# A hybrid encoder block on one core: some steps of the gated recurrence are put at other places between the projection groups

## The chip, the cores and the metric

The kernel runs on one core of a Trainium2 chip. The metric is the device time of one execution in microseconds (us); lower is better.

## The reference

One layer of a streaming encoder, for x of 2048 positions by 1024 features in f32:

```python
h = _rmsnorm(x, norm1_w[layer])
proj = h @ w_in[layer]                      # 1024 x 2816
qa, ka, va, qb, fb, ib, gb = jnp.split(proj, SPLIT_POINTS, axis=-1)
ya = _swa_sink_attention(qa, ka, va, ...)   # 8 query heads, 2 key heads, band of 128
yb = _hgrn2(qb, fb, ib, gb, ...)            # 4 heads of a gated linear recurrence
x = x + jnp.concatenate([ya, yb], axis=-1) @ w_out[layer]
h = _rmsnorm(x, norm2_w[layer])
gate, up = jnp.split(h @ w_gate_up[layer], 2, axis=-1)
x = x + (jax.nn.silu(gate) * up) @ w_down[layer]
```

The change is in the part of `_hgrn2`. Per head it makes, for chunks of 64 positions:

```python
b = jnp.cumsum(jnp.log(fg), axis=3)
att = einsum(qh * exp(b - ref), kh * exp(ref - b))    # causal scores inside a chunk
d_state = einsum(kh * exp(b_last - b), vh)            # what each chunk adds to the state
state = decay * state + d_state                       # a scan over the chunks
o = _rmsnorm(att @ vh + (qh * exp(b)) @ state, g_norm_w) * silu(g)
```

## The kernel before

There are two phases. The first (0 to about 885 us) computes the projection, the banded attention, the recurrence and the output projection; the second is the feed-forward part, and the change leaves it alone.

The first phase goes through 4 blocks of 512 positions (`b` = 0 to 3). A block is one list of steps, `STEPS`, made by `block_steps`. Its backbone is the projection: weight chunks with the names KV, QA0, QA1, F0, F1, Q01, I01, G01, F23, Q23, I23, G23, then WO0 to WO3 for the output projection. Each chunk is cut in 2 or 4 groups; a group is 24 matmuls on TensorE (L208 to L210, eight tiles with three products each) into one of two banks `a_pj`. The call `after(chunk, group, steps...)` lists by hand what comes between one group and the next. Below "G01,3" is group 3 of chunk G01.

Every engine has a loop of its own over the same list, and does its share of each step in this order. An engine never takes a later step first: if its instruction waits, all that is listed behind it waits too. The steps of the recurrence for a head h, and who works in them:

- `ha`: VectorE scales the gate (L952), ScalarE takes its logarithm (L605).
- `hb`: VectorE makes the running sum and the differences (L956, L958, L961, L966), then ScalarE five exponentials (L610 to L615).
- `hc`: VectorE four products (L971, L972, L974, L975). `kt` and `att` of the head wait for the last of them.
- `kt`: TensorE transposes `a_k_end` into a bank `a_tr` (L814), ScalarE copies it to `a_k_nat` (L651).
- `ds` (listed twice for a head, because it fills two banks; the work is done at the second): TensorE makes the state increments from `a_k_nat` and `a_i_nat` (L826), and VectorE scans them into `a_state` and `a_carry`: a copy (L1015) and eight dependent instructions that read the banks (L1019).
- `att`: TensorE makes the scores into `a_hb` (L806), VectorE copies them masked into `a_att_m` (L1011).
- `o`: TensorE multiplies scores and state by the values (L833, L838). `on1`, `on2`, `on3` normalize, `yt` transposes the result.

Of the attention there are: `sm1` (softmax: maxima on VectorE, L984 to L989, exponentials on ScalarE, L634 and L636), `sm2` (the division on VectorE, L993 to L997), `pt` (TensorE transposes the probabilities, L787, ScalarE copies them, L642) and `pv` (TensorE, L797; ScalarE L646, VectorE L1002). The weights of a chunk are rounded by ScalarE (`split_hi`, L518), and VectorE makes what is left (`split_lo`, L855). Where they have no place of their own in the list, those of the next chunk stand ahead of group 0 for the chunks of two groups, F23 among them, and behind it for the chunks of four. The evacuation of each projection group is ScalarE's, in the step of the group itself (L576 for F, L578 for Q, L581 for G, L591 for I).

The steps `qT`, `pt`, `kt`, `ds`, `yt` and `xT` take turns in two banks `a_tr`, in the order of the list. Ahead of each, TensorE waits until the bank has been read by whoever uses it two turns earlier; for `ds` that reader is the scan, which tells it with its last instruction:

```python
def bank_read(b, use):
    if use >= 2:
        read, index = tr_read[TR_USES[use - 2][0]]
        pe.wait_ge(read.sem, read.upto(b, index(TR_USES[use - 2])))

tr_read = {..., "pt": (probT_ready, ...), "kt": (k_nat_ready, ...), "ds": (state_ready, ...), ...}
```

And `ds` waits for the copy of the keys and for the values, which for heads 2 and 3 means all four groups of chunk I23:

```python
if par == 0:
    pe.wait_ge(k_nat_ready.sem, k_nat_ready.upto(b, h + 1))
    pe.wait_ge(i_ready.sem, i_ready.upto(b, TT if h < 2 else 2 * TT))
bank_read(b, use)
```

The loads of weights on SyncE's queue wait for `split_lo` of two chunks earlier. GpSimd has the small powers for the normalizations, and some loads and stores.

Of the kernel before, what the change touches and what calls it, by code (L numbers as in the profile page):

```python
# [57 lines left out]
def chunk_name(n):  # L58
    return CHUNKS[n][0] if n < len(CHUNKS) else f"WO{n - len(CHUNKS)}"


def chunk_groups(n):

    name = chunk_name(n)
    return CHUNKS[n][2] // P if name in FIRST_HEAD else TT
# [4 lines left out]
CHUNK_AT = {chunk_name(n): n for n in range(NW)}  # L70


def block_steps():

    at = {}

    def after(name, group, *steps):
        at.setdefault((name, group), []).extend(steps)

    after("KV", 3, ("vmix",))
    after("QA1", 0, ("qn1", 0))
    after("QA1", 1, ("qn1", 1))
    after("QA1", 2, ("qn1", 2), ("qn2", 0))
    after("QA1", 3, ("qn1", 3))
    after("F0", 0, ("qn2", 1), ("split_hi", CHUNK_AT["Q01"]), ("split_lo", CHUNK_AT["Q01"]), ("qn2", 2))
    after("F1", 0, ("qn2", 3))
    after("Q01", 0, ("qT", 0), ("qT", 1), ("qT", 2), ("qT", 3), ("kT",))  # L90
    after("Q01", 1, ("sc", 0), ("sm1", 0), ("sm1", 1))
    after("I01", 0, ("ha", 0), ("split_hi", CHUNK_AT["G01"]))
    after("I01", 1, ("sm2", 0), ("sm2", 1), ("sc", 1), ("split_lo", CHUNK_AT["G01"]))
    after("I01", 2, ("pt", 0), ("pt", 1), ("sm1", 2), ("sm1", 3), ("hb", 0))
    after("I01", 3, ("sm2", 2), ("sm2", 3), ("pv", 0), ("sc", 2))
    after("G01", 0, ("pt", 2), ("pt", 3), ("sm1", 4), ("sm1", 5), ("xload",), ("hc", 0), ("ha", 1))
    after("G01", 1, ("sm2", 4), ("sm2", 5), ("pv", 1), ("split_hi", CHUNK_AT["F23"]), ("split_lo", CHUNK_AT["F23"]))
    after("G01", 2, ("pt", 4), ("pt", 5), ("sc", 3), ("att", 0), ("kt", 0), ("sm1", 6), ("sm1", 7), ("hb", 1))
    after("G01", 3, ("ds", 0, 0), ("ds", 0, 1), ("sm2", 6), ("sm2", 7), ("pv", 2), ("hc", 1))
    after("F23", 0, ("pt", 6), ("pt", 7))  # L100
    after("F23", 1, ("pv", 3), ("o", 0), ("on1", 0), ("kt", 1), ("ha", 2), ("sq", 0))
    after("Q23", 0, ("on2", 0), ("on3", 0), ("hb", 2), ("split_lo", CHUNK_AT["I23"]), ("ds", 1, 0), ("ds", 1, 1), ("att", 1))
    after("Q23", 1, ("yt", 0), ("hc", 2), ("sq", 1))
    after("I23", 0, ("o", 1), ("on1", 1), ("ha", 3))
    after("I23", 1, ("on2", 1), ("on3", 1), ("split_lo", CHUNK_AT["G23"]), ("kt", 2), ("sq", 2))
    after("I23", 2, ("yt", 1), ("att", 2), ("sq", 3))
    after("I23", 3, ("hb", 3),)
    after("G23", 0, ("ds", 2, 0), ("ds", 2, 1), ("hc", 3), ("n1a",))
    after("G23", 1, ("o", 2), ("on1", 2), ("kt", 3), ("n1b", 0), ("n1b", 1))
    after("G23", 2, ("on2", 2), ("ds", 3, 0), ("ds", 3, 1), ("att", 3))  # L110
    after("G23", 3, ("on3", 2), ("o", 3), ("on1", 3), ("yt", 2), ("n1b", 2), ("on2", 3), ("on3", 3), ("n1b", 3))
    for n in range(CHUNK_AT["WO0"], NW):
        after(chunk_name(n), 1, ("split_lo", n + 1))
    after("WO0", 0, ("xT", 0))
    after("WO0", 1, ("xT", 1))
    after("WO0", 2, ("xT", 2))
    after("WO1", 0, ("xT", 3))
    after("WO1", 2, ("xT", 4))
    after("WO2", 0, ("xT", 5))
    after("WO2", 2, ("xT", 6))  # L120
    after("WO3", 0, ("xT", 7))

    placed = [step for group in at.values() for step in group if step[0].startswith("split")]
    steps = []
    for n in range(NW):
        first_steps = [part for part in (("split_hi", n + 1), ("split_lo", n + 1)) if part not in placed]
        for g in range(chunk_groups(n)):
            if (chunk_name(n), g) == ("WO0", 0):
                first_steps.append(("yt", HG - 1))
            if g == 0 and (chunk_groups(n) < TT or chunk_name(n) == "WO0"):  # L130
                steps += first_steps
            steps.append(("proj", n, g))
            steps += at.pop((chunk_name(n), g), [])
            if g == 0 and not (chunk_groups(n) < TT or chunk_name(n) == "WO0"):
                steps += first_steps
    assert not at, at
    return steps


STEPS = block_steps()  # L140


# [1475 lines left out]
```

## Time and profile before

| | us |
|---|---|
| median of 3 runs | 2302.94 (2302.03 to 2303.75) |
| the profiled execution | 2303.67 |
| its span, first to last instruction | 2301.9 |
| TensorE busy | 2199.6 |
| VectorE busy | 1261.1 |
| ScalarE busy | 928.7 |
| mean granted TensorE clock | 0.984 |

The span is the time in which the profile shows instructions; the time of the execution has 1.8 us more around it. "Busy" counts the time in which an instruction of the engine runs. Start times below are counted from the beginning of the span, and the four blocks of the first phase look alike: the same step lies some 218 us later in the next block.

### The profile page before, as it was taken

What the parts mean: (1) busy time and instruction counts of PE and PEld (TensorE: products, weight loads), DVE (VectorE), ACT (ScalarE), POOL (GpSimd) and SP (SyncE); (2) the same over time, 40 slices, a digit from 0 to 9 for tenths busy, and PEclk for the clock granted to TensorE, in tenths of its full rate; (3) what the DMA queues carried; (4) which work ended last, traced back from release to release, by engine and by line L of the source; (5) the groups of instructions that cost most, each with busy time, mean ns of one, the idle gap of its engine ahead of it and who ended that gap; (6) DMA issues with size and microseconds to landing.
All of it is one profiled execution on the core that took longest, in us unless ns stands there. A gap on an engine that the chain in (4) does not pass through costs nothing.

```text
span 2301.9 us, 31427 instructions
## 1 busy us (share of the span) xinstructions
PE 2199.6 (96%) x12640; PEld 1903.9 (83%) x12640; DVE 1261.1 (55%) x1902; ACT 928.7 (40%) x1674; POOL 143.9 (6%) x154
## 2 busy tenths in 40 slices
PE   7999999999999993699999999999999999999999
PEld 7889988998898893588888888888888788888887
DVE  4675466447635754556666566555555334343333
ACT  4773386448535741333333333333333222232222
POOL 2001201010112002100000000000000000000000
PEclk9999999999999997799999999999999999999999
DMA  3412332323133125623334233222221435445453
GB/s 133 146 58 102 119 112 74 129 92 112 56 138 119 56 93 189 240 84 133 133 133 151 83 137 119 83 82 83 83 83 65 150 139 187 178 180 186 172 193 134
DMA packets 81648, 284.00 MB, mean 123 GB/s; under 512 B 8608, under 2 KB 17056, under 8 KB 66912
## 3 DMA queue, kind: packets, MB, share of 16 engines
q1 hardware_dynamic: 67296, 221.96, 27.2%
q0 software_dynamic: 14208, 60.04, 7.1%
q8 instruction: 100, 1.64, 0.3%
q14 instruction: 44, 0.36, 0.0%
HBM read 227.44 MB, written 54.53 MB: 122 GB/s over the span
## 4 chain that ended last, share of the span: by engine, by line
PE 58%; DMA 2%; DVE 1%; issue 0%; DVEq 0%; POOL 0%; ACT 0%; SPq 0%; POOLq 0%
PE b_bank_A L209 3%; PE b_bank_A L208 3%; PE b_bank_C L209 3%; PE b_bank_B L209 3%; PE b_bank_B L208 3%; PE b_bank_B L210 3%; PE b_bank_A L210 3%; PE b_bank_C L208 3%; PE b_bank_C L210 3%; PE b_hx_bank L1400 3%; PE b_hx_bank L1402 3%; PE b_hx_bank L1401 3%; PE b_bank_D L208 2%; PE b_bank_D L209 2%; PE b_bank_D L210 2%; PE b_hx_bank L1349 1%
## 5 line engine op out<-in xcount | busy, mean ns | idle before, releaser
L1418 DVE TENSOR_TENSOR b_dn_lo<-b_dn_stage,b_dn_hi 128x1024 fp32r<-128x1024 f32 x88 | 107.8, 1226 | 303.8 <-ACT b_dn_hi L1302 303.7
L208 PE MATMUL a_pj<-a_w_hi,a_hT_hi 128*128 128x256 f32 x896 | 259.0, 289 | 1.7 <-issue 1.7
L209 PE MATMUL a_pj<-a_w_lo,a_hT_hi 128*128 128x256 f32 x896 | 253.3, 283 | 0.0
L210 PE MATMUL a_pj<-a_w_hi,a_hT_lo 128*128 128x256 f32 x896 | 253.3, 283 | 0.0
L1302 ACT ACTIVATE b_dn_hi<-b_dn_stage 128x1024 fp32r<-128x1024 f32 x88 | 93.3, 1060 | 341.8 <-PE b_bank_D L1402 310.6
L208 PEld LDWEIGHTS a_pj<-a_w_hi,a_hT_hi 128*128 128x128 f32 x896 | 171.6, 191 | 6.8 <-issue 4.4
L855 DVE TENSOR_TENSOR a_w_lo<-a_w_stage,a_w_hi 128x2048 fp32r<-128x2048 f32 (+1 forms) x64 | 137.9, 2155 | 71.2 <-ACT a_w_hi L518 71.2
L209 PEld LDWEIGHTS a_pj<-a_w_lo,a_hT_hi 128*128 128x128 f32 x896 | 171.7, 192 | 0.0
L210 PEld LDWEIGHTS a_pj<-a_w_hi,a_hT_lo 128*128 128x128 f32 x896 | 171.6, 191 | 0.0
L1400 PE MATMUL b_hx_bank<-b_dn_hi,b_a_hi 128*128 128x512 f32 x352 | 138.3, 393 | 4.9 <-DVE b_a_lo L1418 4.8
L1402 PE MATMUL b_hx_bank<-b_dn_hi,b_a_lo 128*128 128x512 f32 x352 | 137.9, 392 | 0.0
L1401 PE MATMUL b_hx_bank<-b_dn_lo,b_a_hi 128*128 128x512 f32 x352 | 137.9, 392 | 0.0
L208 PE MATMUL b_bank_A<-b_h_hi_B,b_w_hi 128*128 128x512 f32 x352 | 137.6, 391 | 0.0
L208 PE MATMUL b_bank_B<-b_h_hi_T,b_w_hi 128*128 128x512 f32 x352 | 137.3, 390 | 0.0
L209 PE MATMUL b_bank_A<-b_h_lo_B,b_w_hi 128*128 128x512 f32 x352 | 137.2, 390 | 0.0
L210 PE MATMUL b_bank_A<-b_h_hi_B,b_w_lo 128*128 128x512 f32 x352 | 137.0, 389 | 0.0
L210 PE MATMUL b_bank_B<-b_h_hi_T,b_w_lo 128*128 128x512 f32 x352 | 137.0, 389 | 0.0
L209 PE MATMUL b_bank_B<-b_h_lo_T,b_w_hi 128*128 128x512 f32 x352 | 136.9, 389 | 0.0
L1335 ACT ACTIVATE b_gate<-b_u 128x512 f32<-128x512 f32 x44 | 27.8, 632 | 241.3 <-DVE b_u L1541 241.3
L518 ACT ACTIVATE a_w_hi<-a_w_stage 128x2048 fp32r<-128x2048 f32 (+1 forms) x64 | 115.3, 1801 | 1.5 <-DMA a_w_stage<-w_whole 1.5
L1418 DVE TENSOR_TENSOR b_w_lo<-b_mixed_w,b_w_hi 128x1024 fp32r<-128x1024 f32 x88 | 107.6, 1222 | 11.5 <-ACT b_w_hi L1277 11.5
L1321 ACT ACTIVATE b_s<-b_bank_C 128x512 f32<-128x512 f32 x44 | 26.4, 600 | 206.3 <-PE b_bank_C L210 206.3
(266 smaller groups left out, 5557.6 us busy)
## 6 DMA issues: line engine op xcount, KB each, us to landing
a_w_stage<-w_whole SPq DMA_DIRECT2D x56, 1024.0 KB, 4.7
b_gu_stage<-w_gu SPq DMA_DIRECT2D x44, 1024.0 KB, 5.2
b_dn_stage<-w_dn SPq DMA_DIRECT2D x88, 512.0 KB, 3.4
a_mid<-b_a SPq DMA_DIRECT2D x88, 256.0 KB, 4.1
b_a_stage<-a_mid SPq DMA_DIRECT2D x88, 256.0 KB, 3.6
b_hx<-hc POOLq DMA_DIRECT2D x14, 1024.0 KB, 5.1
a_x_res<-x_pad POOLq DMA_DIRECT2D x16, 512.0 KB, 4.4
x_mid<-a_x_res POOLq DMA_DIRECT2D x16, 512.0 KB, 3.4
```

Source lines behind the costliest of these rows:

```text
L208: pe.matmul(out, stationary[0](k), moving[0](k), start=(k == 0 and not adds), stop=False, skip_group_check=adds)
L209: pe.matmul(out, stationary[0](k), moving[1](k), start=False, stop=False, skip_group_check=adds)
L210: last = pe.matmul(out, stationary[1](k), moving[0](k), start=False, stop=(k == ends), skip_group_check=adds)
L518: act.activation(w_hi[s][:, :, 0:cols], w_stage[s][:, :, 0:cols], ACT.Copy).then_inc(w_hi_ready.sem, 1)
L855: dve.tensor_tensor(w_lo[s][:, :, 0:cols], w_stage[s][:, :, 0:cols], w_hi[s][:, :, 0:cols].bitcast(F32), ALU.subtract).then_inc(w_lo_ready ...
L1302: act.activation(f.dn_hi[b][:], f.dn_stage[b][:], ACT.Copy).then_inc(f.dn_hi_ready, 1)
L1321: act.activation(f.s5[:], f.bank["C"][:], ACT.Copy).then_inc(f.s5_ready, 1)
L1335: act.activation(f.gate[1][:], f.u2[:], ACT.Silu).then_inc(f.silu_ready[1], 1)
L1400: pe.matmul(f.down[i], f.a_hi[b][:, rows], f.dn_hi[b][:, cols], start=(j == 0), stop=False)
L1401: pe.matmul(f.down[i], f.a_hi[b][:, rows], f.dn_lo[b][:, cols], start=False, stop=False)
L1402: last = pe.matmul(f.down[i], f.a_lo[b][:, rows], f.dn_hi[b][:, cols], start=False, stop=(j == FT - 1))
L1418: dve.tensor_tensor(out, full, hi.bitcast(F32), ALU.subtract).then_inc(ready, 1)
```

## The change

Five steps move in the list of a block; nothing is added or taken out.

- `kt` of head 0 goes from behind G01,2 to behind G01,3.
- `ds` of head 0 goes from behind G01,3 to behind F23,0, where it stands ahead of `pt` 6 and 7.
- `att` of head 1 goes from behind Q23,0 to behind Q23,1.
- `ds` of head 2 goes from behind G23,0 to behind I23,3, where it stands ahead of `hb` of head 3.

```diff
-    after("G01", 2, ("pt", 4), ("pt", 5), ("sc", 3), ("att", 0), ("kt", 0), ("sm1", 6), ("sm1", 7), ("hb", 1))
-    after("G01", 3, ("ds", 0, 0), ("ds", 0, 1), ("sm2", 6), ("sm2", 7), ("pv", 2), ("hc", 1))
-    after("F23", 0, ("pt", 6), ("pt", 7))
+    after("G01", 2, ("pt", 4), ("pt", 5), ("sc", 3), ("att", 0), ("sm1", 6), ("sm1", 7), ("hb", 1))
+    after("G01", 3, ("kt", 0), ("sm2", 6), ("sm2", 7), ("pv", 2), ("hc", 1))
+    after("F23", 0, ("ds", 0, 0), ("ds", 0, 1), ("pt", 6), ("pt", 7))
     after("F23", 1, ("pv", 3), ("o", 0), ("on1", 0), ("kt", 1), ("ha", 2), ("sq", 0))
-    after("Q23", 0, ("on2", 0), ("on3", 0), ("hb", 2), ("split_lo", CHUNK_AT["I23"]), ("ds", 1, 0), ("ds", 1, 1), ("att", 1))
-    after("Q23", 1, ("yt", 0), ("hc", 2), ("sq", 1))
+    after("Q23", 0, ("on2", 0), ("on3", 0), ("hb", 2), ("split_lo", CHUNK_AT["I23"]), ("ds", 1, 0), ("ds", 1, 1))
+    after("Q23", 1, ("att", 1), ("yt", 0), ("hc", 2), ("sq", 1))
     after("I23", 0, ("o", 1), ("on1", 1), ("ha", 3))
     after("I23", 1, ("on2", 1), ("on3", 1), ("split_lo", CHUNK_AT["G23"]), ("kt", 2), ("sq", 2))
     after("I23", 2, ("yt", 1), ("att", 2), ("sq", 3))
-    after("I23", 3, ("hb", 3),)
-    after("G23", 0, ("ds", 2, 0), ("ds", 2, 1), ("hc", 3), ("n1a",))
+    after("I23", 3, ("ds", 2, 0), ("ds", 2, 1), ("hb", 3),)
+    after("G23", 0, ("hc", 3), ("n1a",))
```

## Rows read from the trace of the kernel before

**Rows 1.** The page's busy times: us, share of the span, instructions.

```profile
PE 2199.6 (96%) x12640; PEld 1903.9 (83%) x12640; DVE 1261.1 (55%) x1902; ACT 928.7 (40%) x1674; POOL 143.9 (6%) x154
```

**Rows 2.** TensorE's waits, first phase: line <- releaser: us in all, times, longest.

```profile
PE a_tr L787 <- DVE a_prob L997: 4.4, 8, 0.9
PE a_tr L814 <- ACT a_probT L642: 3.7, 4, 1.1
...
PE a_hb L833 <- DVE a_carry L1019: 2.9, 4, 0.7
...
PE a_tr L814 <- DVE a_q_h L975: 1.7, 4, 0.7
```

**Rows 3.** Timeline of TensorE, block 1, head 0: start, us, what [idle before <-releaser].

```profile
325.82 1.16 PE L806 MATMUL a_hb<-a_q_in,a_f_gate 128*128 128x128 f32 x8
328.09 0.63 PE L814 MATMUL a_tr<-ident,a_k_end 128*128 128x128 f32 x4 [1.11 <-ACT a_probT L642]
331.51 1.16 PE L826 MATMUL a_tr<-a_i_nat,a_k_nat 64*128 64x128 f32 x16
...
339.94 0.66 PE L787 MATMUL a_tr<-ident,a_prob 128*128 128x128 f32 x4 [0.58 <-DVE a_prob L997]
...
341.44 0.48 PE L208 MATMUL a_pj<-a_hT_hi,a_w_hi 128*128 128x512 f32 x1
```

**Rows 4.** Timeline of VectorE over the same stretch.

```profile
335.18 0.22 DVE L1015 COPY a_state<-a_carry 128x128 f32<-128x128 f32 x1
...
338.45 0.35 DVE L1019 SCALAR_TENSOR_TENSOR a_carry<-a_state,a_decay,a_tr 128x128 f32<-128x128 f32 x1
...
340.89 0.68 DVE L1002 TENSOR_TENSOR a_yA_lo<-a_pv,a_yA_hi 128x512 fp32r<-128x512 f32 x1
...
344.06 2.29 DVE L855 TENSOR_TENSOR a_w_lo<-a_w_stage,a_w_hi 128x2048 fp32r<-128x2048 f32 x1
```

**Rows 5.** Timeline of ScalarE over the same stretch.

```profile
339.37 0.59 ACT L646 ACTIVATE a_yA_hi<-a_pv 128x512 fp32r<-128x512 f32 x1
339.85 1.91 ACT L518 ACTIVATE a_w_hi<-a_w_stage 128x2048 fp32r<-128x2048 f32 x1
```

**Rows 6.** Timeline of TensorE, block 1, heads 2 and 3.

```profile
382.61 1.16 PE L826 MATMUL a_tr<-a_i_nat,a_k_nat 64*128 64x128 f32 x16
...
387.56 1.13 PE L833 MATMUL a_hb<-a_i_nat,a_att_m 128*128 128x128 f32 x8 [0.73 <-DVE a_carry L1019]
...
390.05 0.66 PE L814 MATMUL a_tr<-ident,a_k_end 128*128 128x128 f32 x4 [0.33 <-DVE a_q_h L975]
...
395.65 1.13 PE L806 MATMUL a_hb<-a_q_in,a_f_gate 128*128 128x128 f32 x8 [1.00 <-DVE a_y_nat L1029]
```

**Rows 7.** Timeline of ScalarE over the same stretch.

```profile
379.84 0.39 ACT L591 ACTIVATE a_i_nat<-a_pj 128x256 f32<-128x256 f32 x1 [1.62 <-PE a_pj L210]
381.26 0.63 ACT L610 ACTIVATE a_q_in<-a_t_a 128x512 f32<-128x512 f32 x1 [1.04 <-DVE a_k_end L966]
...
383.13 0.61 ACT L615 ACTIVATE a_t_b<-a_t_b 128x512 f32<-128x512 f32 x1
```

**Rows 8.** Timeline of VectorE over the same stretch.

```profile
378.32 0.41 DVE L956 TENSOR_SCALAR a_f_gate<-a_f_gate 128x512 f32<-128x512 f32 x1
...
380.55 0.68 DVE L966 TENSOR_TENSOR a_k_end<-a_t_b 128x512 f32<-128x512 f32 x1
383.82 0.23 DVE L1015 COPY a_state<-a_carry 128x128 f32<-128x128 f32 x1 [2.59 <-PE a_tr L826]
...
387.33 0.69 DVE L971 TENSOR_TENSOR a_q_in<-a_q_in,a_q_h 128x512 f32<-128x512 f32 x1
```

**Rows 9.** A window: length, busy PE PEld DVE ACT POOL, granted clock, DMA share, GB/s.

```profile
1820.00:1840.00 20.00, 15.17 (x56) 12.05 (x55) 5.48 (x6) 4.73 (x6) 0.00 (x0) 0.83 0.52 196
```

**Rows 10.** Timeline of TensorE inside that window.

```profile
1826.79 0.77 PE L1400 MATMUL b_hx_bank<-b_dn_hi,b_a_hi 128*128 128x512 f32 x1 [4.83 <-DVE b_a_lo L1418]
...
1832.05 0.50 PE L1400 MATMUL b_bank_A<-b_dn_hi,b_a_hi 128*128 128x512 f32 x1
```

## The prediction

> **What bounds the kernel now.** I read the page's busy times first: TensorE works 2199.6 of 2301.9 us, VectorE little more than half of it [rows 1]. So almost everything that the other engines do is hidden, and a change of order counts only through what TensorE waits for. I therefore read TensorE's waits in the first phase. Those at places that the change touches are small: the transposes of the probabilities (L787) wait 4.4 us in all, `kt` 3.7 us for the bank and 1.7 us for the products of `hc`, `o` 2.9 us for the scan [rows 2]. Third, the timelines of block 1 put them in their places: `kt` 0 waits 1.11 us behind `att` 0, and `pt` 6 waits 0.58 us behind group F23,0 [rows 3]; `o` of head 2 waits 0.73 us, `kt` 3 waits 0.33 us, `att` 3 waits 1.00 us [rows 6]. The reader is to see how short these are, and that VectorE and ScalarE are nonetheless packed nearly without a break just there: from 335.2 to 346.35 us VectorE has one piece of work behind the other [rows 4]. A step that is put late into such a queue ends late, and the question for each move is who then waits for its end.
>
> **Head 0: what is removed.** `kt` 0 no longer stands behind `pt` 5, so its wait of 1.11 us a block goes (0.9 on the average: 3.7 in 4 [rows 2]). TensorE then reaches the end of group F23,0 early: `att` 0 begins at 325.82 and takes 1.16, `kt` 0 with G01,3 take 331.51 - 328.09 = 3.42, and `pv` 2 with F23,0 take 339.94 - 0.58 - 331.51 - 1.16 = 6.69 us [rows 3]. That makes 337.1 us.
>
> **Head 0: what is added.** Now come `ds` 0, `pt` 6 and `pt` 7 with no group between them. `pt` 6 and 7 take the two banks that `ds` 0 has just filled, and `bank_read` makes them wait for `state_ready`, thus for the last instruction of the scan. Before, the whole of F23,0 lay between. So the time of `pt` 6 is the end of the scan, and that is a matter of VectorE's queue, which I work out row by row.
>
> - ScalarE: behind the evacuation of G01,3 its copy of `kt` 0 is put in. The copy that follows in the list, of the same 512 columns out of a bank, takes 0.59 us and its successor starts 339.85 - 339.37 = 0.48 later [rows 5]; I take 0.52. The copy for `pv` 2 then ends at 339.37 + 0.52 + 0.59 = 340.5 us.
> - `ds` 0 on TensorE waits for this key copy, which is done at about 340.0. TensorE is idle from 337.1 to 340.0, and `ds` ends at 341.2 (1.16 us [rows 3]). This is not the last wait.
> - VectorE: the scan is gone from its place at 335.18, so `sm2` is done early, but `pv` 2 (L1002) must wait for ScalarE's 340.5. It began at 340.89 before [rows 4], so all that follows comes 0.4 us earlier: the four products of `hc` 1, and the `split_lo` of Q23, which stands ahead of group F23,0 in the list and ended at 344.06 + 2.29 = 346.35; now 345.95. Only then comes the scan, from its copy to its last instruction 338.45 + 0.35 - 335.18 = 3.62 us [rows 4]. It ends at 349.6. The `split_lo` itself waits for ScalarE's `split_hi`, 0.5 us later than before, at 339.85 + 0.52 + 1.91 = 342.3, and that is in time.
>
> `pt` 6 then starts near 349.7. Before, from `pt` 6 to F23,1 went 341.44 - 339.94 = 1.50 us, of which about 0.5 was a second wait, for the probabilities of `pt` 7 (4.4 / 4 less 0.58 [rows 2, 3]), that is long over now; I take off 0.2 more, as transposes that wait for nothing overlap, and reach 350.5. F23,1 began at 341.44: it is 9.0 us late, and this already counts the wait that was removed. What comes after in `STEPS` had no wait until `o` of head 2 and is TensorE's own work; nothing gives the 9.0 us back. The four blocks are alike: 36.0 us.
>
> **Head 1.** `att` 1 moves behind Q23,1. VectorE's list is the same as before there, and its masked copy is an instruction like L1002, some 0.7 us [rows 4]. `o` 1 needs it only after `yt` 0 and the group I23,0; a group of 256 columns takes 387.56 - 0.73 - 382.61 - 1.16 = 3.1 us [rows 6]. I cost it at nothing, with I23,0 for cover. Without this cover it would be the copy, 0.7 us a block; the low end is nothing too, since the trace lists no wait for it [rows 2].
>
> **Head 2 and what it does to head 3.** `ds` 2 now waits for the evacuation of I23,3, which starts at 379.84 and takes 0.39 [rows 7], so it begins at 380.35, some 0.7 us after the group: a new wait, instead of the 0.73 at `o` 2. But on VectorE the scan now stands ahead of `hb` 3. In the profile VectorE did `hb` 3 from 378.32 to 381.23, while TensorE was still in the groups, and then sat idle 2.59 us until `ds` 2 [rows 8]. Now it sits in front of the bank: from `ds` on TensorE to the scan took 383.82 - 382.61 = 1.21 us, so the scan runs from 381.55 and the next instruction can start after 387.33 - 383.82 = 3.51, at 385.1. `hb` 3 takes 381.23 - 378.32 = 2.9: 388.0. Then ScalarE's exponentials, 383.13 + 0.61 - 381.26 = 2.5: 390.5 [rows 7]. Then `hc` 3 and `kt` 3: 390.05 - 387.33 = 2.7 from its first product to TensorE's start [rows 6, 8]. `kt` 3 starts at 393.25 instead of 390.05, that is 3.2 us late, after a wait of nearly 4 us. Behind `hc` 3 on VectorE come `split_lo` of WO0 and the normalization of head 2, for which `att` 3 waits; they start as much later, so the shift stays 3.2 us. 4 blocks: 12.8 us. On ScalarE the evacuation of G23,0 stands behind the exponentials; G23,2, the group behind `kt` 3 that needs its bank, starts 2.7 us after them and covers it.
>
> No moved step has an instruction on SyncE's or GpSimd's queues. The weight loads follow `split_lo`, which is 0.4 us earlier in one place and 3.2 later, with TensorE, in the other.
>
> **The clock.** TensorE is idle for some 2.9 and 8.5 us, with only `ds` 0 between. The nearest row is in the second phase: after an idle 4.83 us [rows 10] the 20 us around it have a mean of 0.83, and as the clock has two levels, 2.4 and 1.2 GHz, that is 0.17 x 20 / 0.5 = 6.8 us at the lower [rows 9]. Of these, work filled 1832.05 - 1826.79 = 5.3 us, matmuls of 0.63 instead of 0.39 us [rows 10]; half of it is lost, 2.6 us. The low end is nothing, the high end that all 6.8 us are filled with work: 3.4. I take 2.6, as 8.5 is longer than the idle of the row: 10.4 us in 4 blocks. At `kt` 3 the wait of nearly 4 us is shorter than the row's, and `att` 3 has 1.00 us of wait that would swallow a part; I take half of 2.6 - 1.0: 0.8 a block, 3.2 in all, with bounds 0 and 2.4 a block. The Trainium skill, "TensorE: Matmul & The Clock Gate", HAM oscillation, counts the penalty of a throttled time as that time x (1 - 1.2/2.4). With the 6.8 us of the row this would be 3.4 instead of 2.6 for each stall at head 0, and the sum 3.2 us higher; this trace bears out less, since a part of the half-speed time was idle anyway. The page also says that kernels which stall once in each round of their loop pay anew in each round; the trace has no such repeated stall.
>
> **Sum.** 36.0 + 12.8 + 10.4 + 3.2 = 62.4 us on the profiled 2303.67, that is 2366.1. The median of the runs is 0.73 us lower: 2365.3; I say 2365.
>
> **Rivals.**
>
> - *The clock stays up.* 48.8 us alone: 2351.7. For it speaks that `ds` 0 and short waits keep some activity; against it rows 9. Chance 0.12.
> - *The clock costs more.* 3.4 and 2.4 a block: 48.8 + 23.2, 2374.9. `pt` 6 and 7 are light work to come back with. Chance 0.12.
> - *The shift at head 3 is hidden.* If ScalarE and VectorE got through `hb` 3 and `hc` 3 by 390 us after all; they would have to start `hb` 3 before the scan, against the list. 36.0 + 10.4: 2349.3. Chance 0.07.
> - *Only head 3 counts.* `pt` 6 finds its banks free because the scan is earlier than I place it: 12.8 us, 2315.7. Chance 0.02.
> - *Faster.* No new wait, the old ones go: 3.7 + 2.9 + 1.7 = 8.3 us, 2294.6. It takes VectorE to have ended the scan by 338.2 us, when `ds` 0 would be done on TensorE at the earliest. For it: the same dependency cost nothing before, with the scan's end at 338.8. Against it: 11.4 us of VectorE's queue [rows 4]. It turns at the scan's end: from 340.7 on (341.44 less the 0.8 of `pt` 6 and 7) head 0 loses. Chance 0.03.
>
> **Range and chances.** The likeliest case has 0.64 and by the bounds of the clock 2358 to 2372 of its own. To hold 8 in 10 I reach down to the cases at 2349 and up to 2375, and let a little more for durations that move with contention: 2344 to 2379. A measurement of this kernel tells 0.2% (4.6 us) from no change. Faster by more 0.03, within 0.01, slower 0.96.
>
> **What would show it.** The waits of TensorE should have new rows: L787 for L1019 (`a_carry`), 4 times, near 8.5 us; L826 for L651 (`a_k_nat`), 4 times, near 3 us; L826 for L591, 4 times, 0.7 us; L814 for L975, 4 times, near 4 us. Gone: L814 for L642 and L833 for L1019. VectorE should show `split_lo` of Q23 directly ahead of the scan of head 0, and at head 2 the scan ahead of L956. The mean clock should be below 0.984, with a half-speed stretch in each block. I am wrong if `pt` 6 waits for something else, if the scan of head 0 starts before L855, or if `hb` 3 doesn't come after the scan.

## The result and the profile after

The changed kernel takes 2363.21 us (median of 5 runs, 2360.97 to 2363.58) against 2302.94 (2301.96 to 2303.75, 5 runs): 1.0261 times, 95% interval 1.0247 to 1.0275. That is 60.3 us slower. The forecast was 2365, in a range of 2344 to 2379. The profiled execution has a span of 2361.4 us. All medians here and below are of the runs in the usual state; one run of the kernel under "VectorE's queue at head 0" (2500.39 us, at a granted clock of 0.853) and one of the kernel before (4494.75 us) are left out as slow.

TensorE's waits of the first phase in the changed kernel, as in [rows 2] for before:

```profile
PE a_tr L787 <- DVE a_carry L1019: 31.0, 4, 8.4
PE a_tr L814 <- DVE a_q_h L975: 15.9, 4, 4.2
...
PE a_tr L826 <- ACT a_k_nat L651: 12.1, 4, 3.1
PE a_tr L826 <- issue: 2.1, 4, 0.5
...
PE a_hb L833 <- DVE a_att_m L1011: 1.7, 4, 0.5
```

Three of the four wait groups of [rows 2] have disappeared: L787 for the probabilities, L814 for `a_probT`, L833 for the scan. In their place stand 31.0 us in which `pt` 6 waits for the scan of head 0, 15.9 at `kt` 3 for `hc` 3 (1.7 before) and 12.1 at `ds` 0 for the key copy. These three alone are 59.0 us. They aren't all loss: 15.7 us of waits that the kernel before had are gone against them (those three, `att` 3 for the normalization of head 2 with 3.0, and the 1.7), and two small ones come in, 2.1 us at `ds` 2 and 1.1 us more at L833 for L1011. That is 46.5 us more of waits; the rest of the loss isn't waiting. Next, TensorE in block 1, head 0, to be laid beside [rows 3]:

```profile
342.23 1.16 PE L806 MATMUL a_hb<-a_q_in,a_f_gate 128*128 128x128 f32 x8
...
356.50 2.08 PE L826 MATMUL a_tr<-a_i_nat,a_k_nat 64*128 64x128 f32 x16 [3.13 <-ACT a_k_nat L651]
366.36 1.94 PE L787 MATMUL a_tr<-ident,a_prob 128*128 128x128 f32 x8 [7.78 <-DVE a_carry L1019]
367.95 0.78 PE L208 MATMUL a_pj<-a_hT_hi,a_w_hi 128*128 128x512 f32 x1
...
369.71 0.40 PE L209 MATMUL a_pj<-a_hT_lo,a_w_hi 128*128 128x512 f32 x1
...
374.38 0.65 PE L797 MATMUL a_pv<-a_probT,a_v_even 128*64 128x256 f32 x4
```

The last line is `pv` 3, the first step behind F23,1; in the kernel before it is this:

```profile
347.09 0.65 PE L797 MATMUL a_pv<-a_probT,a_v_even 128*64 128x256 f32 x4
```

VectorE over the same stretch, to be laid beside [rows 4]:

```profile
356.88 0.69 DVE L1002 TENSOR_TENSOR a_yA_lo<-a_pv,a_yA_hi 128x512 fp32r<-128x512 f32 x1 [3.04 <-ACT a_yA_hi L646]
...
360.05 2.28 DVE L855 TENSOR_TENSOR a_w_lo<-a_w_stage,a_w_hi 128x2048 fp32r<-128x2048 f32 x1
362.25 0.22 DVE L1015 COPY a_state<-a_carry 128x128 f32<-128x128 f32 x1
...
365.87 0.35 DVE L1019 SCALAR_TENSOR_TENSOR a_carry<-a_state,a_decay,a_tr 128x128 f32<-128x128 f32 x1
```

Read both from the start of `att` 0, which is 342.23 here and 325.82 in [rows 3]. The scan begins 20.0 us after it, directly behind `split_lo`, and ends at 366.22; `pt` 6 starts 0.14 us later, 24.1 us after `att` 0 (14.1 before), F23,1 25.7 us after it (15.6 before) and `pv` 3 32.2 us (21.3 before). And VectorE is idle for 3.04 us ahead of L1002: it isn't short of time, it has work listed in an order that doesn't suit.

The four blocks are alike but not equal. From the start of `att` 0, F23,1 starts later than before by 9.8, 10.1, 9.7 and 9.8 us in blocks 0 to 3, and `pv` 3 by 11.6, 10.9, 10.5 and 10.6 us: 43.6 us in all at head 0.

Heads 2 and 3 of block 1, TensorE and then VectorE, to be laid beside [rows 6] and [rows 8]:

```profile
403.97 0.36 PE L208 MATMUL a_pj<-a_w_hi,a_hT_hi 128*128 128x256 f32 x1
...
407.61 1.16 PE L826 MATMUL a_tr<-a_i_nat,a_k_nat 64*128 64x128 f32 x16 [0.52 <-issue]
...
420.50 0.89 PE L814 MATMUL a_tr<-ident,a_k_end 128*128 128x128 f32 x4 [3.88 <-DVE a_q_h L975]
...
426.56 1.16 PE L806 MATMUL a_hb<-a_q_in,a_f_gate 128*128 128x128 f32 x8
```

```profile
408.81 0.23 DVE L1015 COPY a_state<-a_carry 128x128 f32<-128x128 f32 x1 [3.10 <-PE a_tr L826]
...
412.32 0.42 DVE L956 TENSOR_SCALAR a_f_gate<-a_f_gate 128x512 f32<-128x512 f32 x1
...
417.79 0.69 DVE L971 TENSOR_TENSOR a_q_in<-a_q_in,a_q_h 128x512 f32<-128x512 f32 x1 [2.54 <-ACT a_t_b L615]
```

VectorE stands idle 3.10 us in front of a scan that can't start, with `hb` 3 (L956) behind it; then `hb` 3, ScalarE's exponentials and `hc` 3 follow, and `kt` 3 waits 3.88 us. `att` 3 comes 6.06 us behind `kt` 3 here, 5.60 before, of which 1.00 was a wait that is gone now [rows 6]. In block 0 it comes 6.72 us behind:

```profile
187.19 1.12 PE L814 MATMUL a_tr<-ident,a_k_end 128*128 128x128 f32 x4 [3.89 <-DVE a_q_h L975]
...
193.91 1.16 PE L806 MATMUL a_hb<-a_q_in,a_f_gate 128*128 128x128 f32 x8
```

From `pv` 3 to `att` 3 the four blocks take 4.3, 3.6, 3.6 and 4.7 us longer than before, 16.2 us in all. Last, the granted clock:

```profile
356.00:370.00 14.00, 5.72 (x30) 5.11 (x31) 8.30 (x15) 5.71 (x7) 0.00 (x0) 0.51 0.22 75
```

The columns are those of [rows 9]. Of these 14 us nearly all, 0.49 x 14 / 0.5 = 13.7, are at 1.2 GHz; TensorE had idled 3.13 us, made `ds` 0 and idled another 7.78. The clock was low before `ds` 0 began, since its 16 matmuls take 2.08 us here and 1.16 in [rows 3].

### The profile page after: what moved, and what is told of

Read it like the earlier page. It is cut to its first block, busy times and chain, and to the rows that moved or that the text cites. A ratio compares the mean times of both kernels' runs of the same rounds, so it can differ in the third digit from the quotient of the medians.

```text
span 2361.4 us, 31427 instructions
## 1 busy us (share of the span) xinstructions
PE 2212.5 (94%) x12640; PEld 1918.6 (81%) x12640; DVE 1262.8 (53%) x1902; ACT 928.9 (39%) x1674; POOL 137.9 (6%) x154
## 4 chain that ended last, share of the span: by engine, by line
PE 56%; DMA 2%; DVE 1%; issue 0%; DVEq 0%; POOL 0%; ACT 0%; SPq 0%; POOLq 0%
PE b_bank_A L210 3%; PE b_bank_B L210 3%; PE b_bank_C L210 3%; PE b_bank_B L209 3%; PE b_bank_C L209 3%; PE b_bank_A L209 3%; PE b_bank_A L208 3%; PE b_bank_B L208 3%; PE b_bank_C L208 3%; PE b_hx_bank L1400 3%; PE b_hx_bank L1402 3%; PE b_hx_bank L1401 3%; PE b_bank_D L208 2%; PE b_bank_D L209 2%; PE b_bank_D L210 2%; PE b_hx_bank L1349 1%
```

## The experiments

### The moves of each head alone

The change moves four steps, not five: `kt` and `ds` of head 0, `att` of head 1, `ds` of head 2. The two of head 0 weren't run apart from each other.

```diff
 e1_head0_alone: of the change, only the lines G01,2, G01,3 and F23,0
 e2_head1_alone: of the change, only the lines Q23,0 and Q23,1
 e3_head2_alone: of the change, only the lines I23,3 and G23,0
```

> Only the moves of head 0: its key transposes behind G01,3 and its state increments behind F23,0, ahead of the probability transposes 6 and 7. Theory (pt 6 waits for the bank until VectorE has ended a scan that now stands behind hc 1 and split_lo): about 9 us a block and some 2 us of half-speed clock, so nearly three quarters of the whole loss: 2302.9 + 44 = 2347 us, with waits of L787 for L1019 of 31 us. Rival (the loss is head 3's, and what is seen at pt 6 is only where it surfaces): under 2320 us.

> Only the scores of head 1 moved behind Q23,1. Theory: covered by group I23,0, nothing changes: 2303 us, within 1 us. Rival (o of head 1 waits for the masked copy): up to 0.7 us a block, 2306 us, with a wait of L833 for L1011 at this head.

> Only the state increments of head 2 moved behind I23,3, ahead of hb 3. Theory (the scan and then hb 3, its exponentials and hc 3 stand one behind the other, so kt 3 starts 3.2 us late): 12.8 us and up to 4 us of clock, 2302.9 + 16 = 2319 us, with waits of L814 for L975 near 16 us in all. Rival (a shift that head 0 brings about, none without it): 2303 us.

| | median us | over before (2302.86) | ratio, 95% interval |
|---|---|---|---|
| head 0 alone | 2349.28 | 46.4 | 1.0200, 1.0183 to 1.0217 |
| head 1 alone | 2302.36 | -0.5 | 0.9998, 0.9989 to 1.0008 |
| head 2 alone | 2321.78 | 18.9 | 1.0081, 1.0066 to 1.0096 |

Both losses exist without the other, and head 1 costs nothing. The waits sit where they should. Head 0 alone has, among TensorE's waits:

```profile
PE a_tr L787 <- DVE a_carry L1019: 32.4, 4, 8.4
...
PE a_tr L826 <- ACT a_k_nat L651: 12.2, 4, 3.2
```

and head 2 alone:

```profile
PE a_tr L814 <- DVE a_q_h L975: 15.9, 4, 4.2
...
PE a_tr L826 <- issue: 2.1, 4, 0.5
```

Added up, the parts are 64.8 us against 60.3 for the whole, 4.5 more. The profiled spans give 47.1 and 15.2 us, together 62.3, against 59.5. The profiled execution of head 2 alone is at the low end of its runs (they go from 2318.93 to 2322.25), so a part of this is variation from run to run. Another part can be seen in the traces: with head 0 alone F23,1 takes 7.59, 6.99, 6.98 and 7.12 us in the four blocks, 1.8 us more in all than in the changed kernel (7.49, 6.43, 6.39 and 6.54). The same stall doesn't cost the same in two kernels.

### VectorE's queue at head 0

The changed kernel with the rounding of Q23's weights behind the scan, in VectorE's list alone; TensorE's list stays the same.

```diff
-    after("F23", 0, ("ds", 0, 0), ("ds", 0, 1), ("pt", 6), ("pt", 7))
+    after("F23", 0, ("ds", 0, 0), ("ds", 0, 1), ("split_lo", CHUNK_AT["Q23"]), ("pt", 6), ("pt", 7))
```

> The changed kernel, with one step moved in VectorE's list alone: split_lo of Q23 goes behind the scan of head 0. Theory (the place in VectorE's queue sets the start of pt 6): the scan ends 2.2 us earlier in each block, pt 6 too: 2363.2 - 9 = 2354 us, and L787's wait for L1019 falls from 31 to about 22 us. Rival (pt 6 waits for something that ScalarE or the key copy sets): 2363 us.

2355.43 us, ratio to before 1.0231 (1.0214 to 1.0248), thus 7.8 us less than the changed kernel. VectorE in block 1:

```profile
355.11 0.68 DVE L975 TENSOR_TENSOR a_q_h<-a_q_h,a_t_b 128x512 f32<-128x512 f32 x1
355.72 0.22 DVE L1015 COPY a_state<-a_carry 128x128 f32<-128x128 f32 x1
...
359.14 0.35 DVE L1019 SCALAR_TENSOR_TENSOR a_carry<-a_state,a_decay,a_tr 128x128 f32<-128x128 f32 x1
359.41 2.28 DVE L855 TENSOR_TENSOR a_w_lo<-a_w_stage,a_w_hi 128x2048 fp32r<-128x2048 f32 x1
```

```profile
PE a_tr L787 <- DVE a_carry L1019: 21.7, 4, 5.8
```

The wait falls by 9.3 us, as expected, and the time by less. F23,1, from its first matmul to the next step, takes 6.60, 7.35, 6.33 and 7.51 us in the four blocks, 0.9 us more in all than in the changed kernel: the clock was low for more of it in two of them. The place in VectorE's list sets the start of `pt` 6; the rival is out.

### The bank

The changed kernel with `pt` 6 and 7 in the two score banks, which are free there. ScalarE's copies (L642) read them there.

```diff
-                    bank_read(b, use)
+                    if u < 6:
+                        bank_read(b, use)
...
-                        last = pe.transpose(tr[use % 2][:, i * P:(i + 1) * P], prob[u % 2][:, i, :], ident[:])
+                        last = pe.transpose((tr[use % 2] if u < 6 else sc[u % 2])[:, i * P:(i + 1) * P], prob[u % 2][:, i, :], ident[:])
```

> The changed kernel, with pt 6 and 7 written to the two score banks, which are free by then, instead of the banks that the increments of head 0 have just filled; steps and order stay. Theory (the wait of pt 6 is for the bank): L787 waits for nothing, F23,1 runs inside the scan, and only o 0 waits for the scan's end near 349.6 on the time axis of before, where it stood near 357 in the changed kernel: 7.5 us a block, and the half-speed stretch shrinks by 1 to 2 us: 2363.2 - 30 - 6 = 2327 us. Rival (VectorE's packed queue makes the data of pt 6 late, whatever the bank): 2363 us.

2332.54 us, ratio 1.0130 (1.0116 to 1.0144): 30.7 us less than the changed kernel; some 6 us of the expected gain didn't come. TensorE in block 1 (this kernel has one line more, so the names are L827, L788, L798 and L834):

```profile
347.05 2.08 PE L827 MATMUL a_tr<-a_i_nat,a_k_nat 64*128 64x128 f32 x16 [3.14 <-ACT a_k_nat L651]
349.06 1.97 PE L788 MATMUL a_sc<-ident,a_prob 128*128 128x128 f32 x8
350.68 0.77 PE L208 MATMUL a_pj<-a_hT_hi,a_w_hi 128*128 128x512 f32 x1
...
357.56 0.65 PE L798 MATMUL a_pv<-a_probT,a_v_even 128*64 128x256 f32 x4
...
358.57 1.16 PE L834 MATMUL a_hb<-a_i_nat,a_att_m 128*128 128x128 f32 x8
```

VectorE's scan in the same block:

```profile
352.81 0.22 DVE L1016 COPY a_state<-a_carry 128x128 f32<-128x128 f32 x1
...
356.44 0.35 DVE L1020 SCALAR_TENSOR_TENSOR a_carry<-a_state,a_decay,a_tr 128x128 f32<-128x128 f32 x1
```

The scan is exactly as late as in the changed kernel, but `pt` 6 no longer waits, and F23,1 covers it: `o` 0 starts 1.8 us after the scan's end. So VectorE's late scan hurts only through the bank. What didn't come is this: `ds` 0, `pt` and F23,1 still run in part at the lower clock, 2.08, 1.62 and 6.88 us instead of 1.16, 0.8 and 5.65, that is 3.0 us in this block. I had expected the clock to cost less than in the changed kernel, and in three of the four blocks it costs more, as `ds` 0 now counts too. The 3.1 us for the key copy stay.

### The order at head 3

The changed kernel with `hb` 3 ahead of `ds` 2. TensorE's and ScalarE's lists stay the same, only VectorE's order turns.

```diff
-    after("I23", 3, ("ds", 2, 0), ("ds", 2, 1), ("hb", 3),)
+    after("I23", 3, ("hb", 3), ("ds", 2, 0), ("ds", 2, 1))
```

> The changed kernel, with hb 3 ahead of the increments of head 2 in the list; both stay behind I23,3, so TensorE's order is the same. Theory (kt 3 is late because hb 3 stands behind the scan on VectorE): the wait of L814 for L975 (15.9 us) and its half-speed stretch go; the scan of head 2 then runs in time VectorE had idle, hc 3 starts near 385.1 on the time axis of before, and the waits at o 2, kt 3 and att 3 (0.73, 0.33, 1.00 us a block) go too, against 0.7 us for the evacuation of I23,3: 2363.2 - 16 - 5.6 = 2342 us. Rival (the early increments themselves, by the evacuation of I23,3 and the bank, make head 3 late): 2360 us or more.

2341.75 us, ratio 1.0171 (1.0156 to 1.0187): 21.5 us less, and the wait of L814 for L975 (15.9 us) is gone from the list; L806 for L1029 and L833 for L1019, which the kernel before has, haven't come back. That is more than the 18.9 us that the moves of head 2 cost: `ds` 2 behind I23,3 is itself no loss, only its place ahead of `hb` 3 is. The same order was then put into the kernel before:

```diff
-    after("I23", 3, ("hb", 3),)
-    after("G23", 0, ("ds", 2, 0), ("ds", 2, 1), ("hc", 3), ("n1a",))
+    after("I23", 3, ("hb", 3), ("ds", 2, 0), ("ds", 2, 1))
+    after("G23", 0, ("hc", 3), ("n1a",))
```

> The kernel before, with the increments of head 2 behind I23,3, but behind hb 3 in the list. Theory: a loss of 0.7 us a block for the evacuation of I23,3 and a gain of up to 2.1 us (o 2, kt 3, att 3): 2302.9 - 5.6 = 2297 us. Rival (only the named waits of o 2 and kt 3 go, att 3 keeps its own): 2301.5 us.

2297.31 us against 2303.08, ratio 0.9977 (0.9968 to 0.9986): 5.8 us faster than before. Half of the change's own idea thus pays, in the other order.

### The clock

The changed kernel with work on TensorE that nobody reads, in the two waits of head 0. The outputs aren't touched by it.

```diff
+        def keep_busy(b, count):
+            pe.wait_ge(exp_ready.sem, exp_ready.upto(b, 8))
+            for i in range(count):
+                pe.matmul(sc[0][:], w_hi[0][:, i % KT, 0:P], hT_hi[:, i % KT, :], start=True, stop=True)
...
+                    if (h, par) == (0, 0):
+                        keep_busy(b, 12)
...
+                        if h == 0:
+                            keep_busy(b, 30)
```

> The changed kernel with extra work on TensorE that nobody reads: 12 matmuls of 512 columns ahead of the increments of head 0, and 30 behind them, in waits of about 3 and 8 us that stay. Theory (part of the loss is the half-speed clock on the work behind the wait): the clock stays full, pt 6, 7 and F23,1 take 0.8 and 5.65 us instead of 1.6 and 6.4 or more, and the end is 1.6 to 2.6 us earlier in each block: 2363.2 - 8 = 2355 us; pt 6 still starts at the end of the scan. Rival (the waits alone make the loss): 2363 us, or more by the added work.

2356.78 us, ratio 1.0234 (1.0219 to 1.0248): 6.4 us less than the changed kernel, with more work done. The window of block 1:

```profile
340.00:376.00 36.00, 33.88 (x200) 27.25 (x199) 19.70 (x39) 20.11 (x50) 1.26 (x1) 1.00 0.17 59
```

`pt` 6 (L792 here) still starts with the scan's end, and F23,1 follows it after 0.82 us instead of 1.59:

```profile
363.04 1.06 PE L792 MATMUL a_tr<-ident,a_prob 128*128 128x128 f32 x8 [1.70 <-DVE a_carry L1028]
363.86 0.47 PE L208 MATMUL a_pj<-a_hT_hi,a_w_hi 128*128 128x512 f32 x1
```

Some 6 us of the 60 are the clock at head 0; the remaining loss of head 0 is the wait proper. (The trace has 7.3 us between `att` 0 and `pv` 3, over the four blocks.)

### A lighter queue

If VectorE's order at head 0 is what counts, then the kernel before should gain by an easier one. VectorE's part of `hb` 1 goes into the idle time that it has behind G01,1, as a step `hbv` of its own; ScalarE's part stays.

```diff
-                elif kind == "hb":
+                elif kind == "hbv" or kind == "hb" and step[1] != 1:
...
-    after("G01", 1, ("sm2", 4), ("sm2", 5), ("pv", 1), ("split_hi", CHUNK_AT["F23"]), ("split_lo", CHUNK_AT["F23"]))
+    after("G01", 1, ("sm2", 4), ("sm2", 5), ("hbv", 1), ("pv", 1), ("split_hi", CHUNK_AT["F23"]), ("split_lo", CHUNK_AT["F23"]))
```

> The kernel before with VectorE's part of hb 1 alone moved behind G01,1; the rounding of F23's weights and all else stay. Theory: the scan of head 0 and sm2 end about 1 us earlier or more, so the waits of pt 6 and 7 (4.4 us in all) go, and kt 0 keeps its 3.7 us: 2303 - 4.4 = 2298.6 us. Rival (pt 6 and 7 wait for ScalarE's exponentials after all): 2303 us.

2296.47 us against 2303.11, ratio 0.9973 (0.9963 to 0.9983): 6.6 us faster. L787 waits for nothing, and the next line of its list is still there:

```profile
PE a_tr L814 <- ACT a_probT L642: 3.7, 4, 1.1
```

The last kernel takes this, the turned order at head 3, and the rounding of F23's weights out of the way of `kt` 0:

```diff
-    after("G01", 1, ..., ("pv", 1), ("split_hi", CHUNK_AT["F23"]), ("split_lo", CHUNK_AT["F23"]))
-    after("G01", 2, ..., ("kt", 0), ("sm1", 6), ("sm1", 7), ("hb", 1))
+    after("G01", 1, ..., ("hbv", 1), ("pv", 1))
+    after("G01", 2, ..., ("kt", 0), ("split_hi", CHUNK_AT["F23"]), ("sm1", 6), ("sm1", 7), ("split_lo", CHUNK_AT["F23"]), ("hb", 1))
```

> e7 and a lighter queue at head 0: VectorE's part of hb 1 goes into its idle time behind G01,1, and the rounding of F23's weights behind kt 0 (split_hi) and behind sm1 7 (split_lo); the increments of head 0 stay where they were before. Theory: kt 0 loses its 1.1 us wait, pt 6 and 7 their 1.0 us, at 0.3 us for F23's late weights: 1.8 us a block more than e7, 2297 - 7 = 2290 us. Rival (ScalarE, not VectorE, is what sets these, and gets later by the moved rounding): 2297 us or more.

2287.28 us against 2303.08, ratio 0.9935 (0.9923 to 0.9947): 15.8 us, faster than either kernel. The moved rounding wasn't run alone; beside the 5.8 and 6.6 us of the other two edits it leaves 3.4, near the 3.7 of the wait at `kt` 0. The waits of its first phase, without the start of the kernel and one of 0.2 us:

```profile
PE a_tr L826 <- issue: 2.1, 4, 0.5
PE a_pj L208 <- issue: 1.7, 3, 0.6
PE a_hb L833 <- DVE a_att_m L1011: 1.7, 4, 0.5
PE a_tr L758 <- ACT a_qT L619: 1.6, 4, 0.4
PE a_tr L689 <- DVE a_y_nat L1034: 1.1, 3, 0.4
```

`kt` 0 now follows `att` 0 without a wait, which is what the change did too; it needn't be moved for it.

## Why the prediction was right

**Head 0, the wait that was removed.** Right: L814 no longer waits for L642, and group F23,0 is over early enough for `ds` 0 to wait 3.1 us (forecast 2.9).

**Head 0, the chain.** Right step by step, counted from the start of `att` 0. L1002 was to come 14.7 us after it and came 14.65; the scan's start was put at 20.1 and was 20.0; `pt` 6 at 23.9 and it was 24.1. That a bank makes `pt` 6 wait is shown by the kernel with other banks, that VectorE's list sets the scan by the kernel with the late rounding. Block 1 has a scan a little longer than the others, 3.97 us instead of 3.62, with a gap of 0.42 us in its middle that the profile puts down to "issue". F23,1 is 25.7 - 15.6 = 10.1 us late there, of which 0.8 is the clock on `pt` 6 and 7: 9.3 where I had 9.0. The other three blocks have 9.0, 8.9 and 9.0, so the sum is 36.2 us where I had 36.0. I had `ds` 0 at 1.16 us and it took 2.08 in three blocks; the scan waited for VectorE's queue, so this cost nothing.

**Head 1.** Right: nothing. I wrote that the trace lists no wait of `o` for the masked copy [rows 2]. It does, two of 0.6 us in all, but both are at head 3:

```profile
PE a_hb L833 <- DVE a_att_m L1011: 0.6, 2, 0.4
```

In the changed kernel these are four, 1.7 us, again at head 3; with head 1 alone they are still 0.6, with head 2 alone 1.7. So they belong to the move of head 2, and 1.1 us of the loss was in no term of mine.

**Heads 2 and 3.** Right in the mechanism and in size. From the start of I23,3 to `kt` 3 it is 420.50 - 403.97 = 16.5 us. In the kernel before the group starts here, in block 1:

```profile
376.68 0.36 PE L208 MATMUL a_pj<-a_w_hi,a_hT_hi 128*128 128x256 f32 x1
```

That is 390.05 - 376.68 = 13.4 us ahead of its `kt` 3 [rows 6], so the shift is 3.2 us, as forecast, and it is the same in the other blocks: 12.6 us against 12.8. The kernel with head 2 alone measured 15.2 us by its span and 18.9 by its median, for 12.8 + 3.2 = 16.0 in the forecast. The releaser of the new wait at `ds` 2 was to read L591, and the profile says "issue", with 0.5 us where I had 0.7.

**The clock.** The mechanism right, the size at head 0 too high. I took 2.6 us a block there. `pt` 6 and 7 took 1.59 us in each of the four blocks and F23,1 7.49, 6.43, 6.39 and 6.54; at full clock they take 0.8 and 5.65. That is 33.2 - 25.8 = 7.4 us in all instead of 10.4, and the kernel kept busy gained 6.4. In block 1 TensorE's matmuls were at full speed again some 3 us after its return to work (366.36 to the matmuls behind 369.38, which take 0.40 us), where the row I used had 5.3 [rows 10]. At head 3 the clock did fall after an idle 3.88 us, for which I gave half a chance, and it did so in every block. From `kt` 3 to `att` 3 it makes 1.12, 0.46, 0.46 and 1.54 us more than before, 3.6 us in all (3.2 forecast). The slow work itself is 6.7 us, from the 4.55 us that the stretch takes where nothing waits; the wait of 1.00 us at `att` 3 that three blocks had before swallows 3.0 of it.

**The sum.** By the traces it is 36.2 + 7.4 = 43.6 at head 0, 12.6 + 3.6 = 16.2 at head 3, and 1.1 at L833, together 60.9 us. The first matmul of the second phase comes 61.0 us later than before:

```profile
942.95 3.68 PE L1349 MATMUL b_hx_bank<-ident,b_hx 128*128 128x128 f32 x16 [58.33 <-DMA b_hx<-hc]
1003.94 3.68 PE L1349 MATMUL b_hx_bank<-ident,b_hx 128*128 128x128 f32 x16 [58.29 <-DMA b_hx<-hc]
```

(The first line is of the kernel before, the second of the changed one.) The span grew by 59.5, so 1.5 us came back in the second phase, and why wasn't followed up. The forecast 62.4 was 2 us too high. A part of this closeness is luck: the clock at head 0 was 3.0 us too high, and the 1.1 at L833 and 0.4 at head 3 that were missing made up for half of it.

The Trainium skill, "TensorE: Matmul & The Clock Gate", HAM oscillation, would count half of the throttled time: with the 13.7 us of the window above, an estimate by it is 6.8 us a block, against a measured 1.6 to 2.6. Most of the low stretch was idle; TensorE is busy for 5.72 of the 14 us. On the other point of that page, that a stall in each round is paid for in each round, the trace agrees: all four blocks show it.

**The rivals.** The clock staying up, the hidden shift, head 3 only, and the faster case are each ruled out by a wait or a run of their own above. The costlier clock didn't come. The 2358 to 2372 that I gave the likeliest case can't be had from its terms: the bounds I set for the clock give 2351.7 to 2374.9, which the stated range holds as well.

## What to carry to other kernels

When a step is moved, write down, for every engine, what now stands ahead of its share and what stands behind it, and who takes its buffer next: here TensorE's order looked harmless, and the cost came from one scan that landed behind a weight rounding, and from a bank that the very next step wanted. Work that waits for a result of the bound engine should stand behind work in the same queue that is ready: turning two entries of one line was worth 21.5 us in the changed kernel, and the move of `ds` 2, which had cost 18.9 us ahead of `hb` 3, gained 5.8 behind it. A wait of the bound engine costs more than its length once the clock falls, but only for the work that then runs slowly, not for the idle part.

## What the runs showed that I had not expected

- The clock fell after idle times of 3.88 us too, not only after 4.83 as in [rows 10], and in three blocks of the changed kernel it was low after the 3.13 us ahead of `ds` 0. It came back after 3 us of work in one block, while in block 0 F23,1 took 7.49 us instead of 5.65. The same stall costs 1.6 us in one block and 2.6 in another.
- A wait that is removed can give back more than its length. In the kernel with `hb` 1 early the named waits of `pt` 6 and 7 were 4.4 us. The 6.6 us of its time don't show this, as their interval goes from 3.9 to 8.5, but the trace does: from `att` 0 to `pv` 3 the four blocks take 6.2 us less than before. `pt` 6 to F23,1 takes 0.80 us there, 1.50 in [rows 3] with a second wait of 0.43. Transposes that don't wait overlap with each other and with what is around them.
- The scan, eight dependent instructions of VectorE after a copy, showed a gap of 0.42 us in its middle in one of its sixteen passes in the first phase, head 0 of block 1 (one of 0.22 us, head 3 of block 0, the kernel before has too). It is 0.44 us in the kernel kept busy too, where TensorE wasn't idle, so that isn't the reason. Its cause stays open.
